# Twenty-four modulation products taken out of the weight ring and done in six whole pieces, attention items turned three ahead instead of two

## What is computed

```python
shift, scale, gate = split(silu(c) @ w_mod[l] + b_mod[l], 3)        # and the same for the context's c
h  = rmsnorm(x, norm_g[l]) * (1 + scale) + shift
f_in, f_gate, g_u, g_v, g_gate, c_q, c_kv, k_rope, a_gate = split(h @ w_in[l])
f  = (fft2(f_in).real @ w_fmix) * silu(f_gate)                      # groups of 64 columns
g  = g_u * (g_ws @ layernorm(g_v) + g_bs) * silu(g_gate)
q  = rope(rmsnorm(rmsnorm(c_q) @ w_uq)); k, v from c_kv and k_rope  # 8 heads of 96 and 64
o  = softmax(q @ k.T / sqrt(96)) @ v * silu(a_gate)
x  = x + gate * (concat(f, g, o) @ w_out[l])
```

## Time and profile before

| | us |
|---|---|
| three runs | 985.42, 979.25, 978.74 |
| median | 979.25 |
| the profiled execution, its time | 986.22 |
| the profiled execution, its span | 984.4 |
| mean granted TensorE clock | 0.965 of full |

### The profile page before, as it was taken

How to read it: one execution, slowest core, us unless ns; L and a number is a source line. 1 busy time by engine, 2 the same in 40 slices (tenths; PEclk the granted TensorE clock), 3 DMA queues, 4 the chain that set the end, 5 groups by cost and what they waited for, 6 DMA issues and landing times.

```text
span 984.4 us, 14348 instructions
## 1 busy us (share of the span) xinstructions
PE 910.2 (92%) x5858; PEld 746.5 (76%) x5858; DVE 628.2 (64%) x1242; ACT 430.2 (44%) x721; POOL 0.2 (0%) x4
## 2 busy tenths in 40 slices
PE   5899999999899799997999999898989799999994
PEld 1577666565478677764998888788888799999993
DVE  3454764644645749656679998976677755555554
ACT  3262143433533345345444444365543644444432
POOL 0000000000000000000000000000000000000000
PEclk9899999999799799999999999999999899999997
DMA  9560133434413133242556665442455256556531
GB/s 356 220 208 1 43 111 103 150 106 155 136 43 104 42 118 129 86 155 93 152 193 185 201 183 159 129 129 66 128 148 174 76 182 192 185 161 209 166 95 43
DMA packets 39954, 135.71 MB, mean 138 GB/s; under 512 B 4432, under 2 KB 5584, under 8 KB 39760
## 3 DMA queue, kind: packets, MB, share of 16 engines
q1 hardware_dynamic: 39024, 130.48, 40.8%
q10 hardware_dynamic: 864, 4.32, 1.2%
HBM read 133.73 MB, written 1.05 MB: 137 GB/s over the span
## 4 chain that ended last, share of the span: by engine, by line
PE 75%; DVE 16%; ACT 5%; DMA 3%; issue 1%; SPq 0%; ACTq 0%; DVEq 0%
PE ps L350 13%; PE ps L351 12%; PE ps L355 11%; PE ps L448 3%; PE ps L422 3%; PE ps L421 3%; PE ps L420 3%; PE ps L666 3%; DVE wlo L1339 3%; PE ps L689 2%; DMA raw<-wpack 2%; DVE AF L1800 2%; PE ps L353 2%; PE ps L868 1%; PE ps L506 1%; PE ps L674 1%
## 5 line engine op out<-in xcount | busy, mean ns | idle before, releaser
L350 PE MATMUL ps<-hh,whi 128*128 128x256 f32 (+1 forms) x1032 | 310.6, 301 | 3.7 <-DVE AF L1845 2.6
L351 PE MATMUL ps<-hl,whi 128*128 128x256 f32 (+1 forms) x1032 | 305.5, 296 | 0.0
L1339 DVE TENSOR_TENSOR wlo<-raw,whi 128x1024 fp32r<-128x1024 f32 (+3 forms) x206 | 234.1, 1150 | 62.7 <-ACT whi L898 62.5
L898 ACT ACTIVATE whi<-raw 128x1024 fp32r<-128x1024 f32 (+3 forms) x206 | 205.0, 997 | 151.2 <-DMA raw<-wpack 70.4
L355 PE MATMUL ps<-hh,wlo 128*128 128x256 f32 (+1 forms) x897 | 265.6, 296 | 0.0
L350 PEld LDWEIGHTS ps<-hh,whi 128*128 128x128 f32 x1032 | 198.9, 193 | 15.3 <-issue 9.0
L351 PEld LDWEIGHTS ps<-hl,whi 128*128 128x128 f32 x1032 | 199.1, 193 | 5.0 <-issue 0.7
L355 PEld LDWEIGHTS ps<-hh,wlo 128*128 128x128 f32 x897 | 173.1, 193 | 4.0
L420 PE MATMUL ps<-whi,hh 128*128 128x512 f32 (+1 forms) x192 | 70.7, 368 | 0.8 <-ACT wk L998 0.8
L421 PE MATMUL ps<-wlo,hh 128*128 128x512 f32 (+1 forms) x192 | 70.2, 366 | 0.0
L422 PE MATMUL ps<-whi,hl 128*128 128x512 f32 (+1 forms) x192 | 70.2, 366 | 0.0
(11 more groups left out here) (254 smaller groups left out, 1275.9 us busy)
## 6 DMA issues: line engine op xcount, KB each, us to landing
raw<-wpack SPq DMA_DIRECT2D x196, 512.0 KB, 4.1
AF<-wmod SPq DMA_DIRECT2D x16, 512.0 KB, 10.3
raw<-wpack SPq DMA_DIRECT2D x16, 448.0 KB, 4.1
raw<-wpack SPq DMA_DIRECT2D x24, 256.0 KB, 2.8
XT<-xin SPq DMA_DIRECT2D x4, 512.0 KB, 6.1
raw<-wpack SPq DMA_DIRECT2D x4, 432.0 KB, 3.3
uq<-wuq ACTq DMA_DIRECT2D x2, 768.0 KB, 5.1
cst<-cpack ACTq DMA_DIRECT2D x1, 1093.0 KB, 7.9
```

What stands on the lines that cost most here:

```text
L350: e.matmul(o, wh[:, b], xh(k), start=j == 0, stop=False, skip_group_check=True)
L351: e.matmul(o, wh[:, b], xl(k), start=False, stop=False, skip_group_check=True)
L898: e.activation(W.hi(i), W.raw(i), ACT.Copy).then_inc(*HI.up(j))
L1339: e.tensor_tensor(W.lo(i), W.raw(i), W.hi(i), ALU.subtract).then_inc(*LO.up(j))
```

## The change

- `MODS0`'s six pieces leave the ring (`WTOTAL` shrinks by 24 chunks of 1024 columns, so later chunks move up). Each quarter gets a place of its own (`mslot`): parts of `ag`, `ug` and `Pb`, areas of layer 0 that are unused before its attention. One set of four places serves all six pieces: SP's new `mods(q)` waits until PE is done with piece q - 1, then copies four quarters of 512 KB.
- PE does a piece whole (`mod_piece(q)`: four `mod_g`, then the transposes of the piece before), at six points between the second projection and `kv_proj(1)`. ACT's `row` and DVE's `bias` follow at fitting points. In the loop of layer 0 no modulation is left.
- SP issues `mods` between ring chunks: chunk 17 stands behind `mods(2)`, chunk 18 behind `mods(3)`, chunk 19 and all later ones behind `mods(5)`.
- Attention: `Pb` has four places instead of three; `turned(i - 3)` and, on odd turns, `values(i - 5)`; one turn more, four begun output projections; `BESIDE`'s projections are cut in halves on two turns, later than before; `LATE` is 27 and 14 instead of 22 and 10.

```diff
 def mod_g(l, n, g):
-            c, w, _ = weights((*key, g), ("w_mod", l, (2 * g, 2 * g + 1), (512 * n, 512)), 1024, split=False)
+        elif (l, n) in MODS0:
+            pe.wait_ge(K.mw_in[g]["in", MODS0.index((l, n))])
+            w = K.mslot(g)
+        else:
+            c, w, _ = weights((*key, g), ("w_mod", l, (2 * g, 2 * g + 1), (512 * n, 512)), 1024, split=False)
+    def mod_piece(q):
+        for g in range(4):
+            mod_g(*MODS0[q], g)
+        if q:
+            mod_t(*MODS0[q - 1])
...
             for i in range(len(FIRST)):
                 first(i, 1)
+                if i == 1:
+                    mod_piece(0)
+            mod_piece(1)
...
         ps.drop(st)
+        if l == 0:
+            mod_piece(2)
...
+            else:
+                mod_piece(3)          # after w12, before vf
...
             inp("fgate", 1)
+            if l == 0:
+                mod_piece(4)
...
+            mod_piece(5)
             kv_proj(1)
+            mod_t(1, 1)
...
-        for i in range(ni + 3):
+        for i in range(ni + 4):
...
-            if 0 <= i - 2 < ni:
-                turned(i - 2)
-            if i - 3 > 0 and i % 2 == 0:
-                values(i - 4)
+            if 0 <= i - 3 < ni:
+                turned(i - 3)
+            if i >= 5 and i % 2:
+                values(i - 5)
...
-LATE = (22, 10)
+LATE = (27, 14)
-    return max(8 * (t - 2 * l) + 10, LATE[l] + 2 + t % 2)
+    return max(8 * (t - 2 * l) + 11, LATE[l] + 2 + t % 2)
-BESIDE = ({0: ("agate", 0), 2: ("agate", 1), 4: ("agate", 2), 6: ("agate", 3), 9: ("ggate", 0), 12: ("gu", 0), 15: ("ggate", 1), 18: ("gu", 1), 20: ("gws", 0)},
-          {0: ("agate", 0), 1: ("agate", 1), 3: ("agate", 2), 4: ("agate", 3), 6: ("gu", 1), 8: ("gws", 0)})
+BESIDE = (halves(*(("agate", m, 2 * m, 2 * m + 1) for m in range(4)), ("ggate", 0, 9, 11), ("gu", 0, 13, 15), ("ggate", 1, 17, 19), ("gu", 1, 21, 23), ("gws", 0, 25, 25)),
+          halves(*(("agate", m, 2 * m, 2 * m + 1) for m in range(4)), ("gu", 1, 9, 11), ("gws", 0, 12, 12)))
...
+    def mods(q):
+        for g in range(4):
+            sp.wait_ge(K.mm[("mod", *MODS0[q - 1])] if q else K.mm["mod", 0, 1])
+            e.dma_start(K.mslot(g), K.wmod[16 + 4 * q + g].rearrange("p (k n) -> p k n", k=2)).then_inc(*K.mw_in[g].up(("in", q)))
...
-    chunks(6, len(W.plan))
+    chunks(6, 11)
+    mods(0)
+    chunks(11, 15)
+    mods(1)
+    chunks(15, 17)
+    mods(2)
+    chunks(17, 18)
+    mods(3)
+    chunks(18, 19)
+    mods(4)
+    mods(5)
+    chunks(19, len(W.plan))
```

More of the change, by code:

```diff
@@ L697, in layer @@
         mt = lambda k: V[l, "mix", k]
-        steps = list(MODSTEPS0) if l == 0 else mod_order(((1, 4), (1, 5)))
-        for i in range(ni + 3):
+        steps = mod_order(MODS1) if l else []
+        half = None
+        for i in range(ni + 4):
             if i < ni:
@@ L722, in layer @@
                     M.mark(("hread", l))
+                elif a == 0:
+                    half = lin_first((l, nm, m), "w_in", l, (OFF[nm] + P * m, P), 4, xh, xl, N, ht)
                 else:
-                    inp(nm, m)
+                    lin_rest(half, xh, xl, N, ht)
             if i >= ni:
@@ L954, in scalar_program, with mod_row @@
         first_h(k)
+    def mod_row(q):
+        row(*MODS0[q], MODS0[q - 1] if q else (0, 1))
     def layer(l):
@@ L1128, in layer @@
         ni = len(items)
-        steps, prev = (list(MODSTEPS0), (0, 1)) if l == 0 else (mod_order(((1, 4), (1, 5))), (1, 1))
-        for i in range(ni + 3):
+        steps, prev = mod_order(MODS1) if l else [], (1, 1)
+        for i in range(ni + 4):
             if i < ni:
                 exps(i)
-            if i - 1 in BESIDE[l]:
-                beside(*BESIDE[l][i - 1])
+            if i - 1 in BESIDE[l] and (BESIDE[l][i - 1][2] or BESIDE[l][i - 1][0] == "gws"):
+                beside(*BESIDE[l][i - 1][:2])
             if l == 0 and i == 0:
@@ L1477, in layer @@
         V.mark((l, "tab"))
+        if l == 0:
+            bias(0, 4)
         st = ps.ap((l, "st"), 8)
@@ L1512, in fourier @@
                 lows((l, "fgate", 0))
+            else:
+                bias(1, 2)
             for t in tiles:
@@ L1604, in layer @@
         if l == 0:
+            bias(0, 5)
             hsum("k", 0, 0, 0, 0)
@@ L1614, in layer @@
             fourier()
+            bias(1, 3)
             dft()
@@ L1619, in layer @@
                 heads_T("q", 0, 1, y)
+            bias(1, 0)
             kv_take(1, 0, M[l, "kT", 0, 1, 4])
+            bias(1, 1)
         else:
@@ L1740, in layer @@
                 mod_step(*steps.pop(0))
-            if 0 <= i - 3 and items[i - 3][1] == 7:
-                out_gate(items[i - 3][0])
+            if 0 <= i - 4 and items[i - 4][1] == 7:
+                out_gate(items[i - 4][0])
             if i in BESIDE[l] and BESIDE[l][i][0] != "gws":
-                lows((l, *BESIDE[l][i]))
+                lows((l, *BESIDE[l][i][:2]))
             for m in range(2):
@@ L2228 @@
     assert at == WTOTAL
-    wmod = np.stack([I["w_mod"][0].reshape(4, 2, P, 3 * D)[g, :, :, 512 * n:512 * n + 512].transpose(1, 0, 2).reshape(P, 1024) for n in EARLY for g in range(4)])
+    pieces = [(0, n) for n in EARLY] + list(MODS0)
+    wmod = np.stack([I["w_mod"][l].reshape(4, 2, P, 3 * D)[g, :, :, 512 * n:512 * n + 512].transpose(1, 0, 2).reshape(P, 1024) for l, n in pieces for g in range(4)])
     r = _run(nc, [{"cpack": cpack, "xin": np.ascontiguousarray(xin), "wpack": wpack, "wmod": wmod,
```

61 lines of the change are left out of this document (40 added, 21 removed).

## The result

The changed kernel takes 988.1 us (median of 9 runs, 987.2 to 995.3), the kernel before 980.05 beside it (median of 9, 978.3 to 985.4). The ratio of the two is 1.0082, its 95% interval 1.0056 to 1.0108. So the change costs 8 us: a loss that can be told from nothing, and a little smaller than the 1% by which the chances were parted; the 0.50 that was given to more than that went to a case that didn't come, and 0.37 to the one that did. Neither is a typical one: the one before took 986.2 us, 6.2 above the median, and the one of the changed kernel 995.3, the longest of its nine and 7.2 above.

What follows compares the result with a forecast made beforehand. PE, busy 92% of the span, was taken as the bound. 32.2 - 17.6 - 2 = 12.6, taken as +12 on span 984.4: 996, profiled 998, median 991; range 970 to 1001, likeliest case 984 to 999.

Steps and rivals of the forecast that it cites:

- First projections, +32.2: First projections: stage grows by 32.2 us, from added piece work, two new PE waits and a half-clock spell.
- Work, +14.4: First projections: six pieces of 2.70 us add 16.2, piece 3 covers an old 1.76 us wait, leaving +14.4.
- First wait: Before kv_proj(0): ACT's lookahead stands for chunk 18, queued behind mods(3), so PE waits 12.4 us.
- Second wait: At fgate 1: ACT's silu first takes chunks 19 and 20, so PE waits 3.7 us for a bank.
- Clock: First projections: one half-clock spell of 3.4 us behind the wait at fgate 1 adds 1.7 us.
- Layer 0's loop, -17.6: Layer 0's attention: 24 quarters leave (-23.5), switches add 0.8, waits and half clock rise 5.1: shrinks 17.6 us.
- Layer 1, -2: Layer 1's attention: most of 4.3 us behind the norm goes, first output projection waits some 3: net -2 us.
- The lookahead never reaches PE: Rival, first projections: without the 16.1 us of the two lookahead waits the time is 975; chance 0.10.
- Faster: Rival: chunk 18 is in time and layer 0's loop gains too, below 969.5, put at 963 us; chance 0.09.
- Three ahead empties the loop: Rival, layer 0's loop: projection waits come, but 15 of its 22 us of waits go: 976; chance 0.18.
- DVE late on every bare turn: Rival: layer 0's loop shrinks by only 3 to 5 us, layer 1 by nothing: 1005; chance 0.10.
- Chunk 18 overtakes: Rival, first projections: chunk 18 lands at 6 us instead of 9, chunk 20 likewise: -5, 986; chance 0.08.

Runs made afterwards that it cites:

- e1: The changed kernel with SP's order alone altered, chunk 18 ahead of mods(3), chunks 19 and 20 ahead of mods(4): 0.9930 of the kernel before, 974.3 us.
- e5: The changed kernel with attention as before (two ahead, whole projections, old places), pieces moved and SP's order kept: 1.0117 of the kernel before.
- e8: e5 with SP's order of e1 (chunk 18 ahead of mods(3), 19 and 20 ahead of mods(4)): 0.9938 of the kernel before.
- e9: e1 with attention put back to two ahead, the projections kept in halves on the new places: 0.9890 of the kernel before.
- e3: The changed kernel, SP's order kept, lookahead of high and low parts cut to two split chunks at layer 0's gvkr and second fgate: 0.9950 of the kernel before.
- e2: The changed kernel with chunk 18 alone issued ahead of mods(3), chunks 19 and 20 left behind mods(5): 0.9973 of the kernel before.
- e6: e1 with DVE's low parts of the mix and first three out tiles a turn later in layer 0: 0.9895 of the kernel before, 969.6 us.

## Why the prediction came out, step by step

991 was forecast and 988.1 measured, within the likeliest case's 984 to 999. The sum was made against the span: +12 there, +9.1 measured. The mechanism of its largest term, ACT's lookahead standing for chunk 18, was right; what was credited to three ahead was not, as said below.

**First projections, +32.2.** From the stretch of the table it is 105.2 - 70.0 = 35.2, and 2.9 of it are the six turns of rows (0.49 each by their rows) that were left out of both sides: 32.2. The terms, with e1 to part them:
- Work, +14.4. In e1, without waits, the stretch is 15.4 longer than before. Take off the 2.9 of turns, add 1.9 that `kv_proj` gained by running at full clock there (4.1 + 4.1 us of L596 and L598 against 5.1 + 5.0): 14.4. Each piece took 2.77 us in the rows, the last 3.56 at half clock.
- First wait, 12.4 taken, 11.66 measured. Chunk 18 was there 8.6 us after the end of piece 2, where I took 9; its high part ends at 105.92, the low part, tables and first half of the bias at 108.23, where I had 12.8 from the piece's end and it was 12.0. DVE's L1529 starts at 108.34, not near 111, since by my sum piece 2 would have ended near 98, and it ended at 96.2. The bank named by hand was the right one: what ended PE's wait was L1413, the bias.
- Second wait, 3.7 taken, 2.78 measured, by the same mechanism: ACT stood for chunk 19, and chunk 20 came 0.18 behind.
- Clock, 1.7 taken. The waits cost 5.3 in e1's light, of which the kernel before already paid 1.9 at `kv_proj`: 3.4. This is the term that was mis-sized, by a factor of two, and the two waits were over by 1.7 together. That the sum is 32.2 again is luck in part: with e5's execution, where the same waits cost 2.4 more and not 5.3, it would have been 29.3.

**Layer 0's loop, -17.6.** It measured -22.6, and -19.7 without the turns. The walk over the turns named the places in the right order, and its total held; the single terms held less well, by up to 2.4 us, so the total is luck in part. PE's timeline gives, with my figures in the order of the turns, 2.78 (I had 1.7), 2.51 (2.4), 0.51 (1.1), 3.14 (2.7), 3.99 (4.2) and 1.32 (3.7), and small ones of 3.1 (1.2): 17.3 us, where I had 17. Four of the rows:

```profile
182.46 1.08 PE L616 MATMUL ps<-cst,AF 128*96 128x128 f32 x8 [2.78 <-DVE AF L1643]
206.32 0.66 PE L720 MATMUL ps<-AF 128*64 128x128 f32 x8 [2.51 <-ACT AF L1166]
...
221.16 1.61 PE L616 MATMUL ps<-cst,AF 128*96 128x128 f32 x8 [3.14 <-DVE AF L1643]
...
277.82 1.98 PE L720 MATMUL ps<-AF 128*64 128x128 f32 x16 [3.99 <-ACT AF L1166]
```

By the sum, -23.5 of quarters, +0.8 of switches and -2.9 of turns leave +3.0 for waits and clock together, where I had +5.1. The waits rose by 6.9 by their rows, so some 4 us went elsewhere. The granted clock doesn't give them (0.93 on the mean against 0.95). The line of the quarters shows 25.3 us of PE busy in the loop before instead of my 23.5, 1.8 of the 4. Most of the rest is work that now comes behind the first output projection, where the stretch ends: it holds 88 transposes of the items (L705) instead of 92 and 160 value products (L720) instead of 176, 0.6 and 1.0 us by their rows. That part is no gain; up to layer 1's first scores the loop is 21.8 shorter.

**What the prediction didn't see** is what this says of the change. I credited the third item with taking away the wait for the norm, and charged `values` to the missing quarters. e5, e8 and e9 show it otherwise: with the quarters gone and two ahead, PE waits 13.7 us in all (12.2 of them for the norm), 3.3 more than with the quarters, and with three ahead 16.8. The wait is set by when DVE and ACT are done with the items, and how far PE looks ahead only says at which instruction it is paid. The sentence that `values(i - 5)` needs the copy of turn i - 1 just as before was the right one, and I drew too little from it.

**Layer 1, -2.** 89.30 us before, 89.10 after: nothing. The 4.3 us behind the norm went to `values` (2.5), to the output projection behind DVE's mix (1.9) and to small ones, as in layer 0.

**The rest, 0.** The 512 us of the fourth window were 4.2 us shorter than the 516 before, but it begins at layer 1's second output projection, the other at the first. From DVE's last low part of layer 1's result on, where nothing was changed, it is 486.0 against 489.0, at a clock of 0.98 against 0.97, and up to the start of the first stretch 57.55 against 58.66. So half-clock spells fall differently from one execution to the next; some 3 to 4 us are the error that a sum against one profiled execution has here, and the 7.2 by which this one lies above its median say that it can be more.

**The rivals.** "The lookahead never reaches PE" was priced at 975 and is what e1 and e3 made of the kernel: 0.993 and 0.995 of 980.05 are 973 and 975. It was not what the kernel as written did. "Faster", 963, wanted the loop to gain with it from having its chunks early; e1's loop is 257.4, no shorter than 255.7, so that half was wrong. "Three ahead empties the loop" is excluded (17.3 us of waits), "DVE late on every bare turn" too: the loop shrank by 19.7, where it had 3 to 5. "Chunk 18 overtakes": it was there 8.6 us after the piece's end, and of the transfers issued from 95 to 108 us it took the longest:

```profile
AF<-wmod SPq DMA_DIRECT2D x4, 512.0 KB, 4.9
raw<-wpack SPq DMA_DIRECT2D x1, 512.0 KB, 6.7
```

(what, count, KB each, median us from issue to landing). No overtaking is to be seen. The Trainium skill (DMA: Bandwidth & Descriptors, Queues, rings and completion order) allows it, since completion is not first in, first out; this run neither needs the rule nor speaks against it.

The burst itself was faster than I took it. I had 352 GB/s from the earlier trace rows; between 98.5 and 104.5 us it moved at

```profile
98.50:104.50 6.00, 0.00 (x0) 0.00 (x0) 0.00 (x0) 0.00 (x0) 0.00 (x0) 0.51 1.00 405
```

405 GB/s with all 16 engines busy. The Trainium skill (Perfetto Trace Analysis, Roofline) states about 435 GB/s as the ceiling of a core's 16 engines; the row agrees, its mean is under it, though single slices of a third of a microsecond read up to 473. By 405 the 2.62 MB take 6.5 us instead of 7.4, about as much as the first wait came out shorter.

## What to carry to other kernels

When transfers are added to a queue that another engine's lookahead also depends on, list for each chunk behind them who asks for it first, not who uses it first. Here ACT asked for a chunk 80 us ahead of its use, stood for it, and held PE through a PSUM bank; moving three chunks up in the order of issues turned +0.8% into -0.7%.
Looking further ahead doesn't shorten a chain that the other engines set; it moves the wait. Look for the instruction that stands idle in the middle of that chain (here a low part waiting 1.26 us for its high part, ahead of a maximum) and put it behind.
Test the parts of a two-part change one at a time: as written, neither part of this one pays alone (1.0102 and 1.0117); the pieces pay once the order of issues is mended (0.9938), and the part that looked helpful is worth nothing.

## What the runs showed of the hardware

After a wait of PE its clock can go on at the lower of its two levels while work is already there again. Both waits of the changed kernel show it, the first in the window behind it, the second in that from 152, where PE is busy throughout at 0.53 (full speed, 1.00, is 2.4 GHz, 0.50 is 1.2):

```profile
103.00:110.00 7.00, 1.63 (x2) 0.84 (x3) 3.78 (x23) 2.97 (x10) 0.00 (x0) 0.50 0.20 80
...
152.00:157.00 5.00, 5.00 (x24) 3.09 (x25) 2.52 (x4) 1.80 (x3) 0.00 (x0) 0.53 0.19 75
```

So 14.4 us of waits cost 19.7 in this execution. The second wait needn't do it. In e5 PE waits 2.71 us at the same place, and works behind it at full clock; there 14.4 us of waits cost 16.9:

```profile
151.23:157.00 5.77, 5.77 (x41) 3.34 (x42) 3.92 (x7) 3.06 (x6) 0.00 (x0) 1.00 0.33 119
```

And the clock fell in a place without a wait as well: in e2 PE is busy for all of 92 to 100 us, through the sums and piece 2, at 0.79 on the mean, where e1 ran the same instructions at 1.00.

```profile
92.00:100.00 8.00, 8.00 (x45) 4.14 (x45) 4.67 (x19) 2.12 (x9) 0.00 (x0) 0.79 0.03 5
```

The kernel before does it too: its `kv_proj(0)`, from 88.36, begins behind the one-column sums without a wait, and from 90 to 92 the clock is 0.50. In e2 as well the fall, from 94 on, comes behind these sums. But e1, e3, e6 and e8 have the same sums and keep 1.00 from 88 to 100. What sets the one apart from the other these runs don't show.
